# Feature-major products with high weights that walk the two halves of an activation tile in turns of two tokens

## The chip, the core and the metric

The kernel runs on one core of one Trainium2 chip, in one launch. The metric is the device time of that core in microseconds, as the median of several runs. TensorE (PE) multiplies: a matmul streams a moving operand of up to 512 columns out of SBUF through a stationary one of 128 columns, and adds the result to a bank of PSUM. VectorE (DVE), ScalarE (ACT) and GpSimd (POOL) do the elementwise work, and 16 DMA engines bring the weights from HBM.

## The reference, cut to what matters

Two blocks on one sequence of 256 tokens, 2048 features wide, in float32. The first mixes three branches (spatial gating, a state-space branch, attention to a memory), the second is a convolution block and a large feed-forward:

```python
proj = h @ w_in                                   # 2048 x 13312
a_u, a_v, a_g, b_x, b_g, x_q, x_g, gate_logits = jnp.split(proj, splits, axis=-1)
...
branch = jnp.einsum('bsnc,ncd->bsnd', ys, w_branch)
merged = jnp.sum(gates * branch, axis=2)
out = merged @ w_out
...
h = h + conformer_conv(hn, ...)                   # h @ w_pw1, taps over time, u @ w_pw2
h = h + jnp.square(jax.nn.relu(hn @ w_up)) @ w_down   # 2048 x 8192 and back
```

Nearly all of the work is products of a [256, 2048] or [256, 1024] activation with a large weight matrix, some 93 million weights in all, each used once.

## The kernel before

**Three products for one.** Each float32 operand is split into a high part, rounded to the type fp32r that TensorE takes, and a low part, the rest. A product is then high weight times high activation, high weight times low activation, and low weight times high activation. An activation is held as `HiLo` (line 275): `pair.hi` and `pair.lo`, tiles of 128 features by 256 tokens, for every 128 features k. `pair.both[:, :, k, :]` is the high and the low tile of one k together. The low tiles lie behind all the high ones, so with 16 tiles the halves of one pair are 4096 elements or 16 KiB apart in each partition; with 8 tiles (the three branch outputs and the gated branch) 8 KiB.

**Chunks.** The weights come in chunks of 128 x 1024 floats, in an order that `plan()` writes down; chunk c goes through ring `raw` (7 slots). ScalarE rounds it into ring `wh` (4 slots, line 730, semaphore `s_hi`), VectorE or GpSimd subtracts to get `wl` (lines 1132 and 661, in place of the raw chunk), and TensorE multiplies. The whole program of TensorE is written in this order, with the small matmuls of the other stages set between chunks.

**Kinds of products.** `chunk(c)` (line 2019) takes them by kind:

- "W", feature-major, the subject here: stages bx, q, k, au, ag, xg, glu, bg, out, p2 and up. The output tile is 128 features by tokens. The stationary operand is the weight tile, the moving one the activation. One `high_products` matmul (line 2005) streams the high and the low tile in one instruction of 512 columns into the two halves of a bank: columns 0 to 255 collect high times high, columns 256 to 511 high times low. One `low_products` matmul (line 2016) of 256 columns adds low weight times high activation to columns 0 to 255. A chunk has eight of each (kk 0 to 7). Every other chunk takes its low products first (`LOW_FIRST`, line 229), so eight or sixteen matmuls of one line stand in a row.
- "M", token-major (lines 2053 to 2055 and 2070 to 2072): the stationary operand is the activation, the moving one 512 adjacent weights, written to a whole bank. Stages av, v, g0, b0, g2, b2, g1, b1 and dn.
- "T" (lines 2087 to 2089): feature-major in three matmuls of 256 columns. The first chunks of bx (line 2122) and p2 (line 2154) have loops of their own, with the same 512-column form as line 2005, and "C" is a convolution with taps.

**Who takes the bank.** When a W tile is complete, ScalarE reads the second half (`half`, line 744) and VectorE adds the first (`add_half`, line 1181). Both read by column, so it matters to them which column holds what, not in which order it was written.

**A strided read elsewhere.** Two short VectorE instructions, lines 1455 and 1456, multiply 32 adjacent values of `V(7)` by 32 values of `tab[:, 1, r, :, 1]`, which are 16 elements or 64 bytes apart in each partition. Lines 1429, 1457 and 1470 are the same instruction with adjacent operands throughout, and line 1320 with 256 adjacent elements. Lines 1345 and 1347 read two elements 16 bytes apart, and line 1673 two adjacent ones.

Of the kernel before, what the change touches and what calls it, by code (L numbers as in the profile page):

```python
# [357 lines left out]
def _build(nc, a, out, ctx):  # L358
# [6 lines left out]
    def at(name, off, n, dt=F32):  # L365
        return nc.alloc_sbuf_tensor_at(name, [128, n], dt, offset=base + off)[:, :]
# [13 lines left out]
    wh = at("wh", o_wh, WN * CH, F32R).rearrange("p (s n) -> p s n", s=WN)  # L380
# [66 lines left out]
    bank = [ctx.enter_context(nc.psum_tensor(f"bank{i}", [128, 512], F32))[:, :] for i in range(8)]  # L447
# [1517 lines left out]
    def tensor(e):  # L1965
# [16 lines left out]
        def ready(per, k):  # L1982
            return k // per + 1 if per else NORMED_FOR[k]
# [13 lines left out]

        def high_products(c, j, i, s, pair, s_act, per, n0):

            dst = bank[j.banks[0]].rearrange("p (h t) -> p h t", h=2)  # L2000
            w.wait_ge(s_hi, HIGH[c])
            for kk in range(8):
                k = 8 * i + kk
                w.wait_ge(s_act, n0 + ready(per, k))
                ins = e.matmul(dst, wh[:, s, kk * 128:kk * 128 + 128], pair.both[:, :, k, :],  # L2005
                               start=i == 0 and kk == 0, stop=i == j.nch - 1 and kk == 7, skip_group_check=True)
            return ins

# [11 lines left out]
        def chunk(c):  # L2020
# [52 lines left out]
            elif j.kind == "W":  # L2073
                if c in LOW_FIRST:
                    low_products(c, j, i, r, pair, s_act, per, n0)
                    ins = high_products(c, j, i, s, pair, s_act, per, n0)
                else:
                    high_products(c, j, i, s, pair, s_act, per, n0)
                    ins = low_products(c, j, i, r, pair, s_act, per, n0)
            else:  # L2080
                dst = bank[j.banks[0]]
                for kk in range(8):
                    k = 8 * i + kk
                    w.wait_ge(s_act, n0 + ready(per, k))
                    lh = wh[:, s, kk * 128:kk * 128 + 128]
                    ll = wl[:, r, kk * 128:kk * 128 + 128]
                    e.matmul(dst[:, 0:T], lh, pair.hi[:, k, :], start=first_part and kk == 0, stop=False)  # L2087
                    e.matmul(dst[:, 0:T], lh, pair.lo[:, k, :], start=False, stop=False)  # L2088
                    ins = e.matmul(dst[:, 0:T], ll, pair.hi[:, k, :], start=False, stop=last_part and kk == 7)  # L2089
# [215 lines left out]
        for c in range(NC):  # L2305
# [4 lines left out]
            if c in (BIAS + 1, BIAS + 3):  # L2310
                h = (c - BIAS) // 2
# [5 lines left out]
            if Z <= c < Z + 4 * Z_STEP and (c - Z) % Z_STEP == 0:  # L2317
# [5 lines left out]
                for g in (2 * i, 2 * i + 1):  # L2323
                    for h in range(2):
                        o = 256 * (g % 2) + 128 * h
                        ins = e.matmul(bank[7][:, o:o + 128], vn[:, h, g * 128:g * 128 + 128], sgw[:, g, :], start=True,
                                       stop=True)
# [11 lines left out]
            if g is not None:  # L2339
                w.wait_ge(s_mg, 4 + g + 1)  # L2340
                w.wait_ge(s_m, 32)
                for n in (2 * g, 2 * g + 1):
                    if n >= 2:
                        w.wait_ge(s_mgl, n - 1)
                    for i in range(4):
                        f, h = n % 2 * 2 + i // 2, i % 2
                        ins = e.transpose(bank[4 + n % 2][:, i * 128:i * 128 + 128],
                                          gate_x[g][:, h, f * 128:f * 128 + 128], ident)
# [35 lines left out]
            if FFN + 6 <= c < FFN + 22 and (c - FFN) % 2 == 0:  # L2384
# [5 lines left out]
                for i in range(4):  # L2390
                    ins = e.transpose(bank[4 + n % 3][:, i * 128:i * 128 + 128],
                                      Xf[:, n // 2 * 4 + i, n % 2 * 128:n % 2 * 128 + 128], ident)
# [109 lines left out]
```

## Time and profile before

| | us |
|---|---|
| median of 3 runs | 1995.88 |
| lowest and highest run | 1995.85, 1995.94 |
| the profiled execution | 1996.44 |
| its span, from first to last instruction | 1994.4 |
| TensorE busy with matmuls | 1979.2 (99%), 11210 matmuls |
| VectorE busy | 1499.2 (75%) |
| ScalarE busy | 967.0 (48%) |
| GpSimd busy | 417.8 (21%) |

The time around the span is 2.0 us. A matmul's duration in the profile includes its way through the array, while the next one is already under way, so that durations of neighbours overlap. What one matmul costs in a stream is the distance from its start to the next start, and that is how the timeline is read below: so many starts between two times.

### The profile page before, as it was taken

The numbers are of one execution on the slowest core, as the hardware profiler recorded it, in microseconds if no ns is written. First come the engines' busy times: TensorE is split into PE (matmuls) and PEld (weight loads), VectorE is DVE, ScalarE is ACT, GpSimd is POOL, SyncE is SP. The second block draws the span as 40 slices with busy tenths as digits, with TensorE's granted clock in tenths as the row PEclk, the third lists the DMA queues.
The fourth block names the chain that finished last, engine by engine and source line by source line (L and its number), as shares of the span: only waits on it lengthen the run. The fifth ranks groups of instructions, "written<-read, shape, count | busy, mean of one in ns | idle before, by whom it ended". The sixth has DMA issues, their size and how long they took to land.

```text
span 1994.4 us, 28447 instructions
## 1 busy us (share of the span) xinstructions
PE 1979.2 (99%) x11210; PEld 1703.0 (85%) x11210; DVE 1499.2 (75%) x2243; ACT 967.0 (48%) x1346; POOL 417.8 (21%) x310
## 2 busy tenths in 40 slices
PE   9999999999999999999999999999999999999998
PEld 8888888888888788888899988888888888888886
DVE  7867888777799976668899996776567557656755
ACT  6555444434444345547643475554444434434443
POOL 0000234333366630000486743000000000000000
PEclk9999999999999999999999999999999999999999
DMA  9765665555665566666566656666666666666664
GB/s 327 230 181 180 186 189 172 160 159 169 181 187 182 179 190 187 192 213 190 158 175 208 191 172 183 188 198 191 191 191 189 193 195 189 192 193 190 190 192 147
DMA packets 105973, 377.45 MB, mean 189 GB/s; under 512 B 11888, under 2 KB 14448, under 8 KB 105712
## 3 DMA queue, kind: packets, MB, share of 16 engines
q1 hardware_dynamic: 105552, 375.10, 61.7%
q8 instruction: 89, 1.46, 0.3%
q10 hardware_dynamic: 288, 0.53, 0.1%
q14 instruction: 44, 0.36, 0.1%
HBM read 372.90 MB, written 2.69 MB: 188 GB/s over the span
## 4 chain that ended last, share of the span: by engine, by line
PE 82%; DVE 13%; ACT 2%; issue 2%; DMA 1%; DVEq 0%; SPq 0%; ACTq 0%
PE bank L2005 23%; PE bank L2016 12%; PE bank L2071 7%; PE bank L2072 7%; PE bank L2070 7%; DVE wl L1132 5%; PE bank L2053 4%; PE bank L2055 4%; PE bank L2054 4%; PE bank L2087 3%; PE bank L2088 3%; PE bank L2089 3%; ACT wh L730 1%; PE bank L2271 1%; DMA raw<-in_w_bxg 1%
## 5 line engine op out<-in xcount | busy, mean ns | idle before, releaser
L1132 DVE TENSOR_TENSOR wl<-raw,wh 128x1024 fp32r<-128x1024 f32 x608 | 759.5, 1254 | 375.9 <-ACT wh L730 374.3
L730 ACT ACTIVATE wh<-raw 128x1024 fp32r<-128x1024 f32 x680 | 714.1, 1057 | 627.7 <-PE bank L2072 226.3
L2005 PE MATMUL bank<-Hr,wh 128*128 128x512 f32 x1536 | 370.6, 392 | 0.2 <-DVE scrB L1181 0.2
L2005 PEld LDWEIGHTS bank<-Hr,wh 128*128 128x128 f32 x1536 | 281.5, 188 | 55.2 <-issue 0.7
L661 POOL TENSOR_TENSOR wl<-raw,wh 128x1024 fp32r<-128x1024 f32 x72 | 174.3, 2430 | 314.0 <-DVE small L1707 245.8
L2070 PE MATMUL bank<-wh,Yr 128*128 128x512 f32 x560 | 217.9, 389 | 0.0
L2071 PE MATMUL bank<-wl,Yr 128*128 128x512 f32 x560 | 217.8, 389 | 0.0
L2072 PE MATMUL bank<-wh,Yr 128*128 128x512 f32 x560 | 217.8, 389 | 0.0
L2016 PEld LDWEIGHTS bank<-Hr,wl 128*128 128x128 f32 x1536 | 197.4, 191 | 8.8 <-issue 1.1
L2005 PE MATMUL bank<-Yr,wh 128*128 128x512 f32 x832 | 201.6, 392 | 0.3 <-DVE gate_b L1202 0.3
L2016 PE MATMUL bank<-Hr,wl 128*128 128x256 f32 x1536 | 200.6, 283 | 0.0
L2005 PEld LDWEIGHTS bank<-Yr,wh 128*128 128x128 f32 x832 | 152.4, 188 | 30.4 <-DVE gate_b L1202 0.5
L2053 PE MATMUL bank<-wh,Hr 128*128 128x512 f32 x384 | 152.1, 396 | 0.1
L2055 PE MATMUL bank<-wh,Hr 128*128 128x512 f32 x384 | 149.6, 390 | 0.0
L2054 PE MATMUL bank<-wl,Hr 128*128 128x512 f32 x384 | 149.5, 389 | 0.0
L2087 PE MATMUL bank<-Hr,wh 128*128 128x256 f32 x448 | 127.5, 284 | 0.2 <-ACT scrB L839 0.2
L2088 PE MATMUL bank<-Hr,wh 128*128 128x256 f32 x448 | 126.8, 283 | 0.0
L2089 PE MATMUL bank<-Hr,wl 128*128 128x256 f32 x448 | 126.8, 283 | 0.0
L2070 PEld LDWEIGHTS bank<-wh,Yr 128*128 128x128 f32 x560 | 105.1, 188 | 21.8
L2071 PEld LDWEIGHTS bank<-wl,Yr 128*128 128x128 f32 x560 | 105.1, 188 | 21.8
L2072 PEld LDWEIGHTS bank<-wh,Yr 128*128 128x128 f32 x560 | 105.1, 188 | 21.8
L1751 DVE SCALAR_TENSOR_TENSOR bank<-upad,cst,bank 128x256 f32<-128x256 f32 x290 | 121.7, 481 | 2.3
(381 smaller groups left out, 2778.1 us busy)
## 6 DMA issues: line engine op xcount, KB each, us to landing
raw<-in_w_up SPq DMA_DIRECT2D x128, 512.0 KB, 3.6
raw<-in_w_dn SPq DMA_DIRECT2D x128, 512.0 KB, 3.5
raw<-in_w_g SPq DMA_DIRECT2D x96, 512.0 KB, 3.6
raw<-in_w_p SPq DMA_DIRECT2D x80, 512.0 KB, 3.7
raw<-in_w_b SPq DMA_DIRECT2D x48, 512.0 KB, 3.6
raw<-in_w_out SPq DMA_DIRECT2D x32, 512.0 KB, 3.6
raw<-in_w_q SPq DMA_DIRECT2D x16, 512.0 KB, 4.1
raw<-in_w_av SPq DMA_DIRECT2D x16, 512.0 KB, 3.6
```

Of the source, the lines that this page charges most:

```text
L730: e.activation(wh[:, c % WN, :], raw[:, c % RAW, :], ACT.Copy).then_inc(s_hi, 1)
L1132: e.tensor_tensor(wl[:, c % RAW, :], raw[:, c % RAW, :], wh[:, c % WN, :].bitcast(F32), ALU.subtract).then_inc(s_low_v, 1)
L2005: ins = e.matmul(dst, wh[:, s, kk * 128:kk * 128 + 128], pair.both[:, :, k, :], start=i == 0 and kk == 0, stop=i == j.nch - 1 and kk == 7, ...
L2016: ins = e.matmul(dst, wl[:, r, kk * 128:kk * 128 + 128], pair.hi[:, k, :], start=False, stop=i == j.nch - 1 and kk == 7, skip_group_check= ...
L2053: e.matmul(dst, xh, rh, start=first_part and kk == 0, stop=False)
L2054: e.matmul(dst, xh, rl, start=False, stop=False)
L2055: ins = e.matmul(dst, xl, rh, start=False, stop=last_part and kk == 1)
L2070: e.matmul(dst, xh, rh, start=first_part and kk == 0, stop=False)
L2071: e.matmul(dst, xh, rl, start=False, stop=False)
L2072: ins = e.matmul(dst, xl, rh, start=False, stop=last_part and kk == 1)
L2087: e.matmul(dst[:, 0:T], lh, pair.hi[:, k, :], start=first_part and kk == 0, stop=False)
L2088: e.matmul(dst[:, 0:T], lh, pair.lo[:, k, :], start=False, stop=False)
```

## The change

One function, `high_products`, is changed, and in it the order of one instruction's columns:

```diff
-            dst = bank[j.banks[0]].rearrange("p (h t) -> p h t", h=2)
+            dst = bank[j.banks[0]].rearrange("p (h u c) -> p u h c", h=2, c=2)
             w.wait_ge(s_hi, HIGH[c])
             for kk in range(8):
...
-                ins = e.matmul(dst, wh[:, s, kk * 128:kk * 128 + 128], pair.both[:, :, k, :],
+                ins = e.matmul(dst, wh[:, s, kk * 128:kk * 128 + 128], pair.both[:, :, k, :].rearrange("p h (u c) -> p u h c", c=2),
```

Before, the moving operand is walked as 256 tokens of the high tile and then 256 of the low one. Now it is walked as two tokens of the high tile, the same two of the low tile, the next two of the high tile and so on: 128 turns of two pairs. The output is walked in the same way, two columns in the first half of the bank, two in the second. Every product lands in the same column as before, and the number of columns, of instructions and of waits is the same.

No instruction moves on any engine. On TensorE only the form of the output differs. In the first chunks of bx, with the matmuls of line 2122 (untouched) ahead and those of lines 2005 (changed) and 2016 (untouched) in turns:

```order
 L2122 MATMUL bank<-Yr,wh 128x512 x8
 L2129 MATMUL bank<-Yr,wl 128x256 x8
-L2005 MATMUL bank<-Yr,wh 128x512 x8
+L2005 MATMUL bank<-Yr,wh 128x128x2x2 x8
 L2016 MATMUL bank<-Yr,wl 128x256 x16
```

Nothing has moved: the same eight matmuls, with their columns in 128 turns of two halves of two tokens.

## Rows read from the trace of the kernel before

**Rows 1.** Page: busy time by engine, granted clock in 40 slices, chain by engine and line.

```profile
PE 1979.2 (99%) x11210; PEld 1703.0 (85%) x11210; DVE 1499.2 (75%) x2243; ACT 967.0 (48%) x1346; POOL 417.8 (21%) x310
...
PEclk9999999999999999999999999999999999999999
...
PE 82%; DVE 13%; ACT 2%; issue 2%; DMA 1%; DVEq 0%; SPq 0%; ACTq 0%
PE bank L2005 23%; PE bank L2016 12%; PE bank L2071 7%; PE bank L2072 7%; PE bank L2070 7%; DVE wl L1132 5%; PE bank L2053 4%; PE bank L2055 4%; PE bank L2054 4%; PE bank L2087 3%; PE bank L2088 3%; PE bank L2089 3%; ACT wh L730 1%; PE bank L2271 1%; DMA raw<-in_w_bxg 1%
```

**Rows 2.** Groups of instructions: form, count, busy us, mean ns, idle before.

```profile
L2005 PE MATMUL bank<-Hr,wh 128*128 128x512 f32 x1536 | 370.6, 392 | 0.2 <-DVE scrB L1181 0.2
...
L2005 PEld LDWEIGHTS bank<-Hr,wh 128*128 128x128 f32 x1536 | 281.5, 188 | 55.2 <-issue 0.7 <-DVE scrB L1181 0.4
...
L2071 PE MATMUL bank<-wl,Yr 128*128 128x512 f32 x560 | 217.8, 389 | 0.0
...
L2005 PE MATMUL bank<-Yr,wh 128*128 128x512 f32 x832 | 201.6, 392 | 0.3 <-DVE gate_b L1202 0.3
...
L2016 PE MATMUL bank<-Hr,wl 128*128 128x256 f32 x1536 | 200.6, 283 | 0.0
...
L2016 PE MATMUL bank<-Yr,wl 128*128 128x256 f32 x832 | 110.3, 283 | 0.1
```

**Rows 3.** Timeline of TensorE, 1862 to 1870 us: start us, us, what, how many.

```profile
1862.48 2.08 PE L2016 MATMUL bank<-Hr,wl 128*128 128x256 f32 x16
1864.39 3.82 PE L2005 MATMUL bank<-Hr,wh 128*128 128x512 f32 x16
1868.05 2.08 PE L2016 MATMUL bank<-Hr,wl 128*128 128x256 f32 x16
```

**Rows 4.** Timeline of TensorE near 1600 us, token-major products.

```profile
1600.46 0.39 PE L2070 MATMUL bank<-wh,Yr 128*128 128x512 f32 x1
1600.69 0.39 PE L2071 MATMUL bank<-wl,Yr 128*128 128x512 f32 x1
...
1604.09 0.39 PE L2071 MATMUL bank<-wl,Yr 128*128 128x512 f32 x1
```

**Rows 5.** Windows: us, busy by engine (count), granted clock, DMA share, GB/s.

```profile
core 0: us, PE busy (x) PEld busy (x) DVE busy (x) ACT busy (x) POOL busy (x), PEclk, DMA share, GB/s
1862.48:1864.39 1.91, 1.91 (x17) 1.91 (x16) 1.84 (x4) 0.00 (x0) 0.00 (x0) 1.00 0.55 217
1864.39:1868.05 3.66, 3.66 (x19) 3.01 (x17) 2.22 (x4) 2.70 (x4) 0.00 (x0) 1.00 0.71 171
1600.46:1604.09 3.63, 3.63 (x18) 3.00 (x16) 2.13 (x2) 1.06 (x1) 0.00 (x0) 1.00 0.63 191
1821.50:1909.00 87.50, 87.50 (x492) 76.79 (x491) 63.24 (x92) 42.52 (x62) 0.00 (x0) 1.00 0.63 189
```

**Rows 6.** Groups of VectorE by form: busy us, mean ns, idle before.

```profile
L1320 DVE TENSOR_TENSOR scrB<-scrB,keep 128x256 f32<-128x256 f32 x64 | 27.2, 425 | 2.2
...
L1455 DVE TENSOR_TENSOR sv<-sv,tab 128x32 f32<-128x32 f32 x1 | 0.2, 211 | 0.0
L1456 DVE TENSOR_TENSOR sv<-sv,tab 128x32 f32<-128x32 f32 x1 | 0.2, 211 | 0.0
L1429 DVE TENSOR_TENSOR sv<-sv 128x32 f32<-128x32 f32 x1 | 0.2, 192 | 0.0
...
L1470 DVE TENSOR_TENSOR sv<-sv 128x32 f32<-128x32 f32 x1 | 0.2, 191 | 0.0
L1457 DVE TENSOR_TENSOR sv<-sv 128x32 f32<-128x32 f32 x1 | 0.2, 189 | 0.0
...
L1673 DVE TENSOR_TENSOR small<-small 128x2 f32<-128x2 f32 x1 | 0.2, 161 | 0.0
...
L1347 DVE TENSOR_TENSOR small<-small 128x2 f32<-128x2 f32 x1 | 0.2, 161 | 0.0
...
L1345 DVE TENSOR_TENSOR small<-small 128x2 f32<-128x2 f32 x1 | 0.2, 157 | 0.0
```

**Rows 7.** Waits: who waited for whom, total us, times, longest us.

```profile
ACT wh L730 <- PE bank L2005: 89.4, 96, 3.0
...
ACT wh L730 <- PE bank L2016: 60.2, 46, 2.7
```

## The prediction

> **What bounds the kernel now.** I read the page first: TensorE is busy for 99% of the span, VectorE for 75%, ScalarE for 48%, the clock is granted in full in every slice, and the chain that ended last goes through PE for 82%, with line 2005, the one that the change touches, at its head with 23% [rows 1]. The groups come next: line 2005 runs 1536 + 832 = 2368 times, its low partner of line 2016 as often, and the idle time before them is 0.6 us in all [rows 2]. So nothing waits for a moment at these matmuls, and each nanosecond that one of them takes more is a nanosecond more at the end. The waits say the same from the other side: ScalarE waits 89.4 and 60.2 us for lines 2005 and 2016 to give back a weight slot [rows 7].
>
> Then the timeline, for the price of one matmul in its stream. Sixteen low products start between 1862.48 and 1864.39: 1.91 us, or 119.4 ns each for 256 columns. Sixteen high products start between 1864.39 and 1868.05: 3.66 us, or 228.8 ns each for 512 columns [rows 3]. Sixteen token-major products, 512 adjacent columns each, take 1600.46 to 1604.09, 3.63 us or 226.9 ns each [rows 4]. From the two steady streams: (226.9 - 119.4) / 256 = 0.420 ns for a column, which is the upper of the two levels of TensorE's clock, 2.4 GHz, as the granted clock of 1.00 in all three windows says [rows 5], and 119.4 - 256 x 0.420 = 11.9 ns that a matmul costs whatever its length.
>
> **The change part by part.** Nothing is removed or added: as many instructions, columns and waits, and the same column gets the same sum, so no other engine's instruction changes its form, order or operands. What changes is the walk. Now the moving operand and the output each jump once in 512 columns. After, they jump at each pair, 255 times, between places 16 KiB apart in SBUF (8 KiB in the branch stages' tiles) and 1 KiB apart in the bank. The change does what it says: the output's form is 128x2x2 per partition, in one instruction.
>
> *One jump.* The high stream has one jump for each matmul and costs 228.8 ns; the token-major one has none and costs 226.9. The 1.9 ns are an upper bound of what one jump costs in the middle. It says little of 255 of them: this jump falls at the end of a tile, where the next piece of memory is a new one anyway.
>
> *A jump at every pair.* No row shows this on TensorE: all its matmuls in this kernel read and write adjacent elements, but for the jump in the middle. So I bound it. Below, it costs nothing, 0 us. A gain from it I can't exclude either, and it is a rival. Above, the nearest row is on VectorE: lines 1455 and 1456 read 32 elements of `tab` that lie 64 bytes apart and take 211 ns, while lines 1429, 1470 and 1457, the same instruction on adjacent elements, take 192, 191 and 189, on average 190.7 [rows 6]. The difference, 20.3 ns for 32 elements, is 0.63 ns each. It isn't a price of the strided form as such, since two elements 16 bytes apart take 157 and 161 ns, where two adjacent ones take 161 (lines 1345, 1347, 1673) [rows 6]. The element itself costs (425 - 190.7) / 224 = 1.05 ns by line 1320 against those of 32. So VectorE gets an element from a new place every 1.05 + 0.63 = 1.68 ns. It would not notice pairs, which it takes in 2.09 ns. TensorE would: it takes a pair in 2 x 0.420 = 0.84 ns. If its reader, too, gets to a new place only every 1.68 ns, a pair costs 1.68 in place of 0.84, and a matmul 256 x 0.84 = 215 ns more: 228.8 + 215 = 444 ns. By 2368 that is **509 us**. With 189 and 192 in place of 190.7 the step is between 1.64 and 1.73 ns, 30 us either way.
>
> I take the upper value, not 0. The ground is the match of sizes: 1.68 ns is twice 0.84, as if the memory gave a piece of 16 bytes every 1.68 ns. A stream of adjacent columns wants exactly that (four columns of 4 bytes, 4 x 0.420 = 1.68 ns), and one that uses half of each piece before it jumps wants twice that. But it is one row of another engine, and a reader that keeps the last piece of both halves would get past it.
>
> *Weighed against the notes.* The Trainium skill, Vector Engine (DVE) Microarchitecture Reference, in the part "The SBUF access granule: adjacent pairs", says that a port keeps its full rate in runs of two adjacent words and that a hop between such runs is free, while a source that hops at every element costs 1.73 ns. The second half agrees with the 1.68 worked out above; the first, carried over to TensorE, would make the term 0 in place of 509 us. What the page doesn't say is whether it holds at TensorE's rate, 2.5 times VectorE's, and no row here shows it.
>
> *Small terms.* The 1.9 ns between the two streams, 2368 x 1.9 = 4.5 us, sit in the first matmuls of a high run after a low run; in a stream twice as slow I expect them to be hidden: -4 us. The weight load of line 2005 takes 188 ns and lies beside the matmul before [rows 2]; under 444 ns it is hidden more deeply. VectorE and ScalarE work 63.24 and 42.52 us of 87.50 in the stage up [rows 5] and get more time for the same work, DMA (0.63 there) too. What is late next is still TensorE. The waits of ScalarE for a slot grow, and nobody waits for that. The token-major, three-matmul and small products don't change.
>
> Sum, on the profiled execution: 1996.4 + 509 - 4 = 2501.4; the median of the runs is 0.6 below that execution: 2501 us, of which I take **2501**.
>
> **The rivals.**
>
> *A, hops between pairs are free: 1996 us.* Each pair is one piece of memory for the reader, and one word pair for the bank, so a new place costs no more than the next one. For it: the jump in the middle costs at most 1.9 ns, and VectorE's row would be just as it is. A finer support would be two pieces held at once, since here two streams alternate, each of which moves on in order. Against it: the size of 1.68 ns. The Trainium skill, Advanced Engine Details and Errata, "Memory Cachelines", states a rule of this kind: two hits on each 16-byte line of SBUF, and every two consecutive elements adjacent in PSUM, are enough; it also says that "Any non-contiguous AP significantly slows down matmuls", which is the other side. By the one the time is 1996, by the other it is well above; no row decides between them. Range 1992 to 2000.
>
> *B, the bank pays and not the reader: 2250 us.* The output adds to what the bank holds, a read and a write for each pair. If two places that follow each other in turns get in each other's way at every second pair, a pair of 0.84 ns is paid once more for every second one: 128 x 0.84 = 107 ns, 2368 x 107 = 254 us. Nothing in the trace speaks for it or against it, since no output jumps more than once. The same slot holds anything between A and my forecast.
>
> *C, slower still: 2760 us.* The array is fed for half of the time in the high runs. If the granted clock falls to the lower level, 1.2 GHz, the high runs lose no more, but the low ones pay 256 x 0.420 = 107.5 ns more each, 2368 x 107.5 = 255 us, and 2501 + 255 = 2756. Against it: the clock stands at 1.00 throughout, and TensorE would still have a matmul under way all the time.
>
> *D, faster: 1991.4 us.* The one thing that a different walk could give back is the 4.5 us of the high runs' first matmuls. If these come from the first half of the bank, which sixteen low products in a row have just written, a high product that goes to the second half at every second pair would meet it half as hard or not at all: 1995.9 - 4.5 = 1991.4. It decides at 0.2%, or 4 us, so only if nearly all of it goes and the hops are free. Against it: it looks like a stream that catches up after short matmuls, whatever they write.
>
> **How the numbers follow.** The forecast, twice the time for the columns of line 2005, has 0.43; its own range is 2445 to 2540: 28 us down where the 11.9 ns of a matmul are hidden too (2368 x 11.9), 30 us down and up from VectorE's rows, and 4 up where the small term stays. A has 0.41, B with all between 0.08, C with all above 0.06, D 0.02. Faster by over 0.2% is D: 0.02. Within 0.2%, about what a measurement of this kernel can tell from no change, is A: 0.41. Slower is the rest: 0.57. For 8 times in 10 the range must hold both the forecast and A. It is 1992 to 2540; C and part of D stay out.
>
> **What would show it.** In the profile after, the start-to-start distance of line 2005 in a run of sixteen: about 440 ns if I am right, 227 to 229 under A, 335 under B. The low products of line 2016 at 119.4 ns say that the clock is untouched; at 227 it is C. Lines 2122 and 2154, unchanged, should keep their distance, and the token-major stages their length. The span of the stage up should grow by the share of its high products, the stage dn not at all. I am wrong if TensorE's reader or the bank holds two places at once, and nothing in this trace can tell.

## The result, and the profile after

The changed kernel takes 2240.72 us (median of 3 runs, 2240.69 to 2241.2) against 1995.88 before: a ratio of 1.1228, with a 95% interval of 1.1206 to 1.125. It is slower by 244.8 us. The direction is the forecast's, the size is not: 2501 us was forecast, and the time came out halfway, where rival B stood with 2250 us. The experiments show that B's mechanism wasn't the reason.

The page of the changed kernel, whose span is 2238.7 us (busy by engine, granted clock, chain by engine and by line):

```profile
PE 2226.2 (99%) x11210; PEld 1723.9 (77%) x11210; DVE 1502.1 (67%) x2243; ACT 973.2 (43%) x1346; POOL 405.9 (18%) x310
...
PEclk9999999999999999999999999999999999999999
...
PE 99%; DVE 0%; ACT 0%; DMA 0%; issue 0%; DVEq 0%; SPq 0%; ACTq 0%
PE bank L2005 35%; PE bank L2016 13%; PE bank L2071 6%; PE bank L2072 6%; PE bank L2070 6%; PE bank L2053 6%; PE bank L2055 6%; PE bank L2054 6%; PE bank L2087 2%; PE bank L2088 2%; PE bank L2089 2%; PE bank L2271 1%; PE bank L2122 1%; PE bank L2149 0%; PE bank L2150 0%; PE bank L2154 0%
```

Against [rows 1], the clock is granted in full throughout as before, TensorE is busy for 99% of a longer span, and the share of line 2005 in the chain goes from 23% to 35%. The chain is now PE for 99%, where it went over VectorE for 13% before: TensorE is so late that nobody else's work comes last. The other engines are busy for the same number of microseconds: VectorE 1502.1 against 1499.2, ScalarE 973.2 against 967.0. So TensorE waits for nothing new; one kind of its instructions takes longer.

The groups of instructions (busy us, mean ns, idle before):

```profile
L2005 PE MATMUL bank<-Hr,wh 128*128 128x512 f32 x1536 | 531.3, 507 | 0.0
...
L2005 PE MATMUL bank<-Yr,wh 128*128 128x512 f32 x832 | 288.2, 507 | 0.0
...
L2071 PE MATMUL bank<-wl,Yr 128*128 128x512 f32 x560 | 217.9, 389 | 0.0
...
L2016 PE MATMUL bank<-Hr,wl 128*128 128x256 f32 x1536 | 202.5, 284 | 0.0
```

Line 2005 has 531.3 + 288.2 us of busy time where [rows 2] had 370.6 + 201.6, 247.3 more. The token-major products of line 2071 have 217.9 (217.8 before) and the low products 202.5 (200.6). The timeline of TensorE in the last stage up, in the form of [rows 3]:

```profile
2110.28 2.10 PE L2016 MATMUL bank<-Hr,wl 128*128 128x256 f32 x16
2112.21 5.49 PE L2005 MATMUL bank<-Hr,wh 128*128 128x512 f32 x16
2117.53 2.10 PE L2016 MATMUL bank<-Hr,wl 128*128 128x256 f32 x16
```

Sixteen high products take 2112.21 to 2117.53, 5.32 us or 332.5 ns each, where they took 228.8. The low ones take 1.93 us, 120.6 ns each, where they took 119.4. 2368 x (332.5 - 228.8) = 245.6 us: the whole difference lies in the start-to-start distance of line 2005. The trace as a whole says the same: from each start to the next start, the 2368 high products take 789.1 us in all, where they took 545.0, which is 244.1 more. In terms of columns: 332.5 less the 11.9 ns that a matmul costs whatever its length is 320.6 ns, or 1.25 ns for each of the 256 pairs, where two columns took 0.84.

The other side of it is seen in the waits. ScalarE, which needs a weight slot back from TensorE, waits longer for line 2005 than in [rows 7]. VectorE in turn waits longer for ScalarE. None of it comes back to TensorE, which has no idle time left before these matmuls:

```profile
ACT wh L730 <- PE bank L2005: 296.7, 135, 4.3
...
ACT wh L730 <- PE bank L2016: 114.5, 59, 2.7
```

### The profile page after: what moved, and what is told of

Same layout as the page of the kernel before. It is cut to its first block, busy times and chain, and to the rows that moved or that the text cites. A ratio compares the mean times of both kernels' runs of the same rounds, so it can differ in the third digit from the quotient of the medians.

```text
span 2238.7 us, 28447 instructions
## 1 busy us (share of the span) xinstructions
PE 2226.2 (99%) x11210; PEld 1723.9 (77%) x11210; DVE 1502.1 (67%) x2243; ACT 973.2 (43%) x1346; POOL 405.9 (18%) x310
## 4 chain that ended last, share of the span: by engine, by line
PE 99%; DVE 0%; ACT 0%; DMA 0%; issue 0%; DVEq 0%; SPq 0%; ACTq 0%
PE bank L2005 35%; PE bank L2016 13%; PE bank L2071 6%; PE bank L2072 6%; PE bank L2070 6%; PE bank L2053 6%; PE bank L2055 6%; PE bank L2054 6%; PE bank L2087 2%; PE bank L2088 2%; PE bank L2089 2%; PE bank L2271 1%; PE bank L2122 1%; PE bank L2149 0%; PE bank L2150 0%; PE bank L2154 0%
## 5 line engine op out<-in xcount | busy, mean ns | idle before, releaser
L2005 PE MATMUL bank<-Hr,wh 128*128 128x512 f32 x1536 | 531.3, 507 | 0.0
L2005 PEld LDWEIGHTS bank<-Hr,wh 128*128 128x128 f32 x1536 | 292.4, 195 | 180.8 <-issue 0.9
L2005 PE MATMUL bank<-Yr,wh 128*128 128x512 f32 x832 | 288.2, 507 | 0.0
L2005 PEld LDWEIGHTS bank<-Yr,wh 128*128 128x128 f32 x832 | 158.3, 195 | 97.0 <-DVE Xf L1304 0.3
L2071 PE MATMUL bank<-wl,Yr 128*128 128x512 f32 x560 | 217.9, 389 | 0.0
L2072 PE MATMUL bank<-wh,Yr 128*128 128x512 f32 x560 | 217.9, 389 | 0.0
L2016 PE MATMUL bank<-Hr,wl 128*128 128x256 f32 x1536 | 202.5, 284 | 0.0
```

The costliest lines, as they stand in the source:

```text
L2016: ins = e.matmul(dst, wl[:, r, kk * 128:kk * 128 + 128], pair.hi[:, k, :], start=False, stop=i == j.nch - 1 and kk == 7, skip_group_check= ...
L2071: e.matmul(dst, xh, rl, start=False, stop=False)
L2072: ins = e.matmul(dst, xl, rh, start=False, stop=last_part and kk == 1)
```

## The experiments

All kernels below are the kernel before with the edit shown. Those with numbers for line 2005 (or 2016) are read like [rows 3], from the starts of sixteen matmuls in a row in the last stage up.

**Which side pays?** The change alters the walk of two operands. The first kernel walks only the moving operand in turns, with the output's columns one behind the other:

```diff
-            dst = bank[j.banks[0]].rearrange("p (h t) -> p h t", h=2)
+            dst = bank[j.banks[0]].rearrange("p (u h c) -> p u h c", h=2, c=2)
...
-                ins = e.matmul(dst, wh[:, s, kk * 128:kk * 128 + 128], pair.both[:, :, k, :],
+                ins = e.matmul(dst, wh[:, s, kk * 128:kk * 128 + 128], pair.both[:, :, k, :].rearrange("p h (u c) -> p u h c", c=2),
```

> Only the moving operand of the high products is walked in turns of two tokens; the output's 512 columns are written one behind the other. This kernel leaves out the sorting of the output: high and low sums lie mixed in the bank, so the numbers are not those of the reference. Theory R (the reader of the moving operand pays for each new place, 106.7 ns for 256 pairs): the distance in a run of line 2005 stays at 333 ns as in the changed kernel, the time near 2241 us. Theory W (the bank pays, the reader nothing): 227 to 229 ns, the time 1996 us. Theory S (the stepping through three dimensions costs on either side, or each side pays a part): between, 280 ns and 2120 us, or 333 in both this run and its counterpart.

Measured: 2240.79 us, ratio 1.1228 (1.1211 to 1.1244). Its timeline:

```profile
2112.06 5.49 PE L2005 MATMUL bank<-Hr,wh 128*128 128x512 f32 x16
2117.38 2.10 PE L2016 MATMUL bank<-Hr,wl 128*128 128x256 f32 x16
```

5.32 us for sixteen, as in the changed kernel. The counterpart leaves the reading as it was and writes in turns:

```diff
-            dst = bank[j.banks[0]].rearrange("p (h t) -> p h t", h=2)
+            dst = bank[j.banks[0]].rearrange("p (g u c) -> p u g c", g=2, c=2)
```

> The counterpart: the moving operand is streamed as before the change, high tile and then low tile, and only the output goes in pairs of columns to the two halves of the bank in turns. It leaves out the right place of the columns, so the numbers are not those of the reference. Theory R (reader): 227 to 229 ns in a run of line 2005 and 1996 us. Theory W (bank): 333 ns and 2241 us. Theory S: as in the counterpart, 280 or 333 ns in both.

Measured: 1995.64 us, ratio 1.0 (0.9991 to 1.0009).

```profile
1863.48 3.82 PE L2005 MATMUL bank<-Hr,wh 128*128 128x512 f32 x16
1867.13 2.08 PE L2016 MATMUL bank<-Hr,wl 128*128 128x256 f32 x16
```

3.65 us for sixteen, as before the change. So the reader of the moving operand pays all of it, and 255 jumps of 1 KiB in the bank cost nothing. Rival B, the bank that meets itself at every second pair, is refuted, though its time of 2250 us was right to 10 us.

**How long must a run be?** The same change with turns of 4, 8, 16 and 128 tokens on both sides; only `c=2` differs in both lines.

> The changed kernel with turns of four tokens in place of two, on both sides, so 127 jumps back and forth in place of 255 and whole pieces of 16 bytes. If each jump costs one step of the array's clock (106.7 ns / 256 = 0.42 ns), a matmul pays 53 ns: 280 ns in a run of line 2005 and 2118 us. If the price comes from pieces of 16 bytes of which only half is used, it is gone: 227 to 229 ns and 1996 us. If the bank pays once for every second pair that goes to another place, whatever lies between, 280 ns or a little less.

> Turns of eight tokens on both sides, 63 jumps. One clock step for each jump: 26.7 ns for each matmul, 253 ns in a run of line 2005, 2057 us. Pieces of 16 bytes: 227 to 229 ns, 1996 us. A threshold anywhere between two and eight tokens also shows as 1996 us here with something else at four tokens.

> The changed kernel with turns of sixteen tokens on both sides. Turns of two, four and eight tokens cost 106.7, 23 and 17 ns for each high product over 226.7. If what is left at four and eight tokens is a price for each jump that shrinks with their number, sixteen (31 jumps) give 8 ns: 235 ns in a run of line 2005 and 2010 us or so. If it is a fixed price of a walk in three dimensions, 17 ns again: 243 ns, 2027 us. If the weights' load takes part (both read the memory in the same rhythm), anything between 227 and 243.

> The changed kernel with turns of 128 tokens: four runs of columns, three jumps, but still a walk in three dimensions. Turns of 4, 8 and 16 tokens cost 23.3, 16.7 and 13.3 ns for each high product over 226.7, which is 10 ns and 0.104 ns for each of the 128, 64 and 32 runs. If the 10 ns come with the walk in three dimensions whatever its runs, 237 ns in a run of line 2005, 2368 x 10.4 = 25 us less the 4.5 of the runs' first matmuls: 2016 us. If they come from something in the short turns, 227 ns and 1996 us.

| tokens in a turn | sixteen high products, us | ns each | time, us | ratio, 95% interval |
|---|---|---|---|---|
| 2 (the change) | 5.32 | 332.5 | 2240.72 | 1.1228, 1.1206 to 1.125 |
| 4 | 4.00 | 250.0 | 2044.91 | 1.0247, 1.023 to 1.0264 |
| 8 | 3.89 | 243.1 | 2026.8 | 1.0155, 1.014 to 1.017 |
| 16 | 3.84 | 240.0 | 2019.06 | 1.0117, 1.0102 to 1.0132 |
| 128 | 3.65 | 228.1 | 1995.58 | 1.0, 0.999 to 1.0009 |
| 256 (before) | 3.66 | 228.8 | 1995.88 | |

The rows of the second and the fifth line of the table:

```profile
1916.33 4.17 PE L2005 MATMUL bank<-Hr,wh 128*128 128x512 f32 x16
1920.33 2.08 PE L2016 MATMUL bank<-Hr,wl 128*128 128x256 f32 x16
```

```profile
1863.39 3.82 PE L2005 MATMUL bank<-Hr,wh 128*128 128x512 f32 x16
1867.04 2.08 PE L2016 MATMUL bank<-Hr,wl 128*128 128x256 f32 x16
```

Nearly all of the price goes from two tokens to four, where a run fills 16 bytes, and not by half, as a price for each jump would. It doesn't vanish there: 21, 14 and 11 ns are left at 4, 8 and 16 tokens. None of the numbers expected for 4, 8 and 16 tokens came out: at 4 tokens the price lies between the 53 ns of a price for each jump and the 0 of whole pieces, and at 16 it lies between the two that were given. At 128 nothing is left, so that it isn't the form of the walk, in three dimensions, that costs.

**Does the distance matter?** The reading turns again, between the high tile of k and that of the next k, 1 KiB away, in place of the low tile 16 KiB away:

```diff
-            dst = bank[j.banks[0]].rearrange("p (h t) -> p h t", h=2)
+            dst = bank[j.banks[0]].rearrange("p (u h c) -> p u h c", h=2, c=2)
...
+            near = 8 * j.nch
...
-                w.wait_ge(s_act, n0 + ready(per, k))
-                ins = e.matmul(dst, wh[:, s, kk * 128:kk * 128 + 128], pair.both[:, :, k, :],
+                w.wait_ge(s_act, n0 + ready(per, min(k + 1, near - 1)))
+                ins = e.matmul(dst, wh[:, s, kk * 128:kk * 128 + 128], pair.hi[:, min(k, near - 2):min(k, near - 2) + 2, :].rearrange("p h (u c) -> p u h c", c=2),
```

> As the run with the reading turns alone, but the second stream is the high tile of the next k, 1 KiB further on, in place of the low tile 16 KiB further on. Left out: high weight times low activation, so the numbers are not those of the reference. If the price is one of the distance (two places 8 or 16 KiB apart that fall in the same part of the memory), it goes down or away: towards 227 ns in a run of the high products and 1996 us. If a pair from a new piece of memory costs 1.25 ns wherever it lies, it stays: 333 ns and 2241 us.

Measured: 2240.66 us, ratio 1.1228 (1.1211 to 1.1244); sixteen products take 5.32 us. The distance has no part in it:

```profile
2112.22 5.49 PE L2006 MATMUL bank<-Hr,wh 128*128 128x512 f32 x16
2117.54 2.10 PE L2017 MATMUL bank<-Hr,wl 128*128 128x256 f32 x16
```

**Turns, or half-used pieces?** The low products have one tile and 256 columns, which allows two walks that the high ones don't. First, turns of two tokens between the halves of the tile, 512 bytes apart:

```diff
-            dst = bank[j.banks[0]][:, 0:T]
+            dst = bank[j.banks[0]][:, 0:T].rearrange("p (h u c) -> p u h c", h=2, c=2)
...
-                ins = e.matmul(dst, wl[:, r, kk * 128:kk * 128 + 128], pair.hi[:, k, :],
+                ins = e.matmul(dst, wl[:, r, kk * 128:kk * 128 + 128], pair.hi[:, k, :].rearrange("p (h u c) -> p u h c", h=2, c=2),
```

> The kernel before, with turns of two tokens in the low products alone (256 columns), between the first and the second 128 tokens of the one high tile, 512 bytes apart; the output in the same turns. Each new pair at 1.25 ns in place of 0.83: 128 x 0.417 = 53 ns more, 173 ns in a run of line 2016, 2368 x 53 = 126 us, 2122 us. If 512 bytes are near enough to be free, or only 512-column instructions pay: 119.4 ns and 1996 us.

Second, always onward, every second pair and then the pairs left out:

```diff
-            dst = bank[j.banks[0]][:, 0:T]
+            dst = bank[j.banks[0]][:, 0:T].rearrange("p (u h c) -> p h u c", h=2, c=2)
...
-                ins = e.matmul(dst, wl[:, r, kk * 128:kk * 128 + 128], pair.hi[:, k, :],
+                ins = e.matmul(dst, wl[:, r, kk * 128:kk * 128 + 128], pair.hi[:, k, :].rearrange("p (u h c) -> p h u c", h=2, c=2),
```

> The kernel before, with the low products' columns taken as every second pair of tokens first (step of 16 bytes) and then the pairs left out: always onward, only one jump back, but each pair in another 16-byte piece. If the price is for a piece of which only half is used before the next, it is the same as in turns: 173 ns in a run of line 2016 and 2122 us. If it is for going back and forth between two places, it is gone: 119.4 ns and 1996 us.

Measured: 2102.56 us (1.0536, 1.052 to 1.0552) for the turns, 2251.15 us (1.128, 1.1262 to 1.1299) for the skipped pairs. The two timelines, the turns first:

```profile
1976.24 2.84 PE L2016 MATMUL bank<-Hr,wl 128*128 128x256 f32 x16
1978.91 3.81 PE L2005 MATMUL bank<-Hr,wh 128*128 128x512 f32 x16
```

```profile
2119.48 3.84 PE L2016 MATMUL bank<-Hr,wl 128*128 128x256 f32 x16
2123.15 3.82 PE L2005 MATMUL bank<-Hr,wh 128*128 128x512 f32 x16
```

Turns: 2.67 us for sixteen, 166.9 ns each, 48 more than 119.4. Skipped pairs: 3.67 us, 229.4 ns each, 110 more, though there is one jump back instead of 127 jumps to and fro. Neither expectation foresaw that the onward walk would cost over twice as much as the turns. It has the very price that the prediction took: (229.4 - 11.9) / 128 = 1.70 ns for each pair. A new theory follows. **TensorE's reader of the moving operand fetches aligned pieces of 16 bytes, one in about 1.68 ns, and keeps the last two.** Skipped pairs need a new piece each: 1.68. In turns between two streams, a pair that opens a piece pays 1.68 and its second half, two pairs later, is still there and pays 0.84: on average 1.26, and 1.25 is what the changed kernel shows. The turns of the low products come a little below it: (166.9 - 11.9) / 128 = 1.21 ns for each pair, 6 ns a matmul less than the 173 that the theory gives, and it doesn't say why.

**Tests of this theory.** Each has a number that it alone gives. Runs of four tokens, with four left out, use whole pieces; the same two tokens later breaks each run over two pieces; four streams in place of two push a piece out before its second half is asked for. The moving operand of line 2016 in the three kernels, in this order (the output is walked in the same way):

```diff
-                ins = e.matmul(dst, wl[:, r, kk * 128:kk * 128 + 128], pair.hi[:, k, :],
+                ins = e.matmul(dst, wl[:, r, kk * 128:kk * 128 + 128], pair.hi[:, k, :].rearrange("p (u e c) -> p e u c", e=2, c=4),
...
+                ins = e.matmul(dst, wl[:, r, kk * 128:kk * 128 + 128], pair.hi[:, k, 2:250].rearrange("p (u e c) -> p e u c", e=2, c=4),
...
+                ins = e.matmul(dst, wl[:, r, kk * 128:kk * 128 + 128], pair.hi[:, k, :].rearrange("p (h u c) -> p u h c", h=4, c=2),
```

> The kernel before, with the low products' columns taken in runs of four tokens with four left out between them, then the ones left out: onward in steps of 32 bytes, each run a whole aligned piece of 16 bytes. Theory P (the reader fetches aligned pieces of 16 bytes, one in 1.67 ns, which is what four columns take; every second pair skipped cost twice): each piece is used whole, so about 120 to 130 ns in a run of line 2016, the time 1996 to 2020 us. Rival J (each step to a place that isn't the next costs, 0.83 ns as with the skipped pairs): 64 steps, 53 ns more, 173 ns and 2122 us.

> As the run with runs of four tokens and four left out, but over tokens 2 to 249, so that each run of four begins in the middle of a 16-byte piece. Left out: the low weights' product for the first two and last six tokens, so the numbers are not those of the reference; 248 columns in place of 256. Theory P (aligned pieces of 16 bytes): each run touches two pieces, 124 pieces x 1.67 ns = 207 ns and what a matmul costs whatever its length, 12 to 17: about 220 ns in a run of line 2016, 2368 x 100 = 237 us more, 2230 us. Rival J (steps cost, wherever a run begins), or pieces that aren't aligned: as the aligned run.

> The kernel before, with the low products' columns taken in turns of two tokens between four streams, 64 tokens or 256 bytes apart, in place of two. Two streams cost 1.25 ns a pair, skipped pairs 1.67. Theory P2 (the reader keeps the pieces it fetched, two of them, so that with two streams every second pair is found there): with four streams each piece is gone before its second half is wanted, 128 x 1.67 = 213 ns and 12 to 17 for the matmul: 228 ns in a run of line 2016, 2250 us. Rival (a jump to another place costs 0.42 ns, however many streams): 166.7 ns and 2103 us as with two.

| walk of the low products | sixteen, us | ns each | time, us | ratio, 95% interval |
|---|---|---|---|---|
| four of eight, aligned | 1.88 | 117.5 | 1991.8 | 0.998, 0.9971 to 0.9989 |
| four of eight, from token 2, 248 columns | 3.54 | 221.3 | 2231.46 | 1.1182, 1.1163 to 1.12 |
| four streams, pairs | 3.60 | 225.0 | 2247.08 | 1.126, 1.1243 to 1.1276 |

```profile
1863.51 2.04 PE L2016 MATMUL bank<-Hr,wl 128*128 128x256 f32 x16
1865.39 3.81 PE L2005 MATMUL bank<-Hr,wh 128*128 128x512 f32 x16
```

```profile
2100.45 3.71 PE L2016 MATMUL bank<-Hr,wl 128*128 128x248 f32 x16
2103.99 3.82 PE L2005 MATMUL bank<-Hr,wh 128*128 128x512 f32 x16
```

```profile
2115.64 3.78 PE L2016 MATMUL bank<-Hr,wl 128*128 128x256 f32 x16
2119.24 3.85 PE L2005 MATMUL bank<-Hr,wh 128*128 128x512 f32 x16
```

The theory of the pieces is close in all three: 120 to 130, 220 and 228 ns were expected, 117.5, 221.3 and 225.0 measured, the first a little below its range. The rivals had 173, about 120 and 167, and are refuted. A shift of 8 bytes (with eight columns fewer) moves the same walk from 1991.8 to 2231.46 us. What the runs do not tell is whether two pieces are kept or three: four streams are too many, two are not. The four streams also lie only 256 bytes apart, a distance that no run tests with two streams. And that pieces are kept is a reading of the times: nothing in a trace shows a fetch.

**Does VectorE, from which the price was taken, behave so?** Three of its instructions in the stage up were walked in other orders, with the same results:

```diff
-                e.tensor_tensor(s, s, keep[1], ALU.mult).then_inc(s_v, w.own())
+                p2 = lambda v: v.rearrange("p (h u c) -> p u h c", h=2, c=2)
+                sk = lambda v: v.rearrange("p (u e c) -> p e u c", e=2, c=2)
+                p1 = lambda v: v.rearrange("p (h u) -> p u h", h=2)
+                e.tensor_tensor(p2(s), p2(s), p2(keep[1]), ALU.mult).then_inc(s_v, w.own())
...
-                e.scalar_tensor_tensor(s, s, 0.0, s, ALU.max, ALU.mult).then_inc(s_hm, 1)
+                e.scalar_tensor_tensor(p1(s), p1(s), 0.0, p1(s), ALU.max, ALU.mult).then_inc(s_hm, 1)
...
-                e.tensor_tensor(hid.lo[:, t % 16, :], s, hid.hi[:, t % 16, :].bitcast(F32),
+                e.tensor_tensor(sk(hid.lo[:, t % 16, :]), sk(s), sk(hid.hi[:, t % 16, :].bitcast(F32)),
```

> The kernel before, with three VectorE instructions of the stage up walked in another order on all operands, 256 columns each, the same results: line 1323 (line 1320 before, 425 ns) in pairs in turns 512 bytes apart, line 1325 (1322 before, 426 ns) in lone elements in turns 512 bytes apart, line 1328 (1325 before, 426 ns) in pairs 16 bytes apart with a pair left out between. By the 1.68 ns for a piece that the prediction took from lines 1455 and 1456: pairs in turns free, 425 ns; pairs with a step free, 426 ns, since a pair takes VectorE 2.09 ns; lone elements 0.63 ns more each if every element needs a fetch, 426 + 161 = 587 ns, and nothing more than 426 if two pieces are kept and the next three elements of each stream are found there. A rival, that VectorE keeps none, gives 587 or more for the lone elements. TensorE has slack to wait for none of them: 1996 us in all cases, up to 2010 if VectorE's longer work falls on its path.

Measured: 1995.49 us, ratio 0.9999 (0.999 to 1.0008). The groups of VectorE, with the lines moved by three:

```profile
L1325 DVE SCALAR_TENSOR_TENSOR scrB<-scrB 128x256 f32<-128x256 f32 x64 | 40.0, 625 | 2.2
...
L1328 DVE TENSOR_TENSOR Yr<-scrB,Yr 128x256 fp32r<-128x256 f32 x64 | 27.3, 427 | 31.0 <-ACT Yr L873 31.0
...
L1323 DVE TENSOR_TENSOR scrB<-scrB,keep 128x256 f32<-128x256 f32 x64 | 27.3, 426 | 2.2
```

Pairs in turns take 426 ns and skipped pairs 427, as adjacent elements do (425 and 426 before): VectorE takes a pair in 2.09 ns, which would leave time for a piece in 1.68. Lone elements in turns take 625 where 426 stood, 0.78 ns each. That is the price of a lone element again (0.63 ns by [rows 6]), or a little more, although each stream comes back to its piece. The expectation that kept pieces make lone elements free is refuted for this instruction. But it names its source twice and also writes in turns, so this run doesn't show which of its reads or writes pays, nor that VectorE keeps no piece where TensorE does.

**What is left, and a better kernel.** The aligned onward walk made the kernel 4.0 us faster than before (1991.8 against 1995.76, measured beside it), where its expectation had 1996 to 2020. More runs look at that. The first walks the moving operand of line 2016 alone; the second has the walk in the low, token-major and three-matmul products; the third and fourth in all products of 256 columns (low and three-matmul ones), in runs of four and of eight. From the second on, each product of the kind is written as here:

```diff
+        sk = lambda v: v.rearrange("p (u e c) -> p e u c", e=2, c=4)
...
-                    e.matmul(dst[:, 0:T], lh, pair.hi[:, k, :], start=first_part and kk == 0, stop=False)
+                    e.matmul(sk(dst[:, 0:T]), lh, sk(pair.hi[:, k, :]), start=first_part and kk == 0, stop=False)
```

> Runs of four tokens with four left out in the low products, on the moving operand alone; the output's columns are written one behind the other. Left out: the right place of the columns, so the numbers are not those of the reference. With both sides walked so, a low product cost 117.8 ns in place of 120.0 and the kernel 1991.8 us. If the 2.2 ns come from the reader: 117.8 ns and 1991.8 us again. If they come from the bank, where a column is then written later than the one beside it: 120.0 ns and 1996 us.

> The same walk (runs of four columns with four left out, then the ones left out), on both sides, in the low products, in all token-major products of 512 columns and in the three-matmul ones of 256 columns; the high products of line 2005 stay as before the change. If a matmul gains 2.2 ns wherever its columns are taken so: 3600 + 1344 more of them, 4944 x 2.2 = 11 us less, 1981 us. If a walk in three dimensions costs 512-column matmuls 10 ns as it does the high products: 3600 x 10 = 36 us more for these and 3 less for the others, 2025 us.

> The version that the experiments point to: the kernel before, with runs of four columns and four left out in all 256-column products of fp32r (low products and three-matmul products, lines 2018 and 2089 to 2091), on both sides. The 512-column products stay as before. The low products gain 2.2 ns each (1991.8 us); with the same walk the three-matmul ones took 53.4, 52.7 and 52.6 us from start to start in place of 54.4, 53.7 and 53.2, which is 2.6 us less: 1989 us. If the gain of the three-matmul ones was only the other stages' shift, 1991.8 us.

> As the run before with runs of eight columns, two whole 16-byte pieces, and eight left out. If what the walk gains comes from taking a piece from another place each time, eight gain half as much or nothing: 117.8 ns becomes 119 to 120 in a run of the low products and the time 1992 to 1996 us. If any onward walk in three dimensions gains it, as with four: 1989 us.

| kernel | time, us | ratio, 95% interval |
|---|---|---|
| reading only, low products | 1991.73 | 0.998, 0.9972 to 0.9989 |
| low, token-major and three-matmul products | 2004.57 | 1.0044, 1.0032 to 1.0057 |
| all 256-column products, runs of four | 1988.88 | 0.9966, 0.9952 to 0.9979 |
| all 256-column products, runs of eight | 1988.57 | 0.9964, 0.9952 to 0.9977 |

The gain lies with the reader (1991.73 us without touching the output's order). It adds up over the 256-column products, and runs of eight give as much as runs of four. For 512 columns the sign turns: the token-major products with this walk, lines 2072 to 2074 there, take 3.70 us for sixteen, 231.3 ns from start to start, where [rows 4] had 226.9. That is 4 ns each, neither the gain of 2 nor the loss of 10 of the expectation, whose 1981 and 2025 us were both missed:

```profile
1609.70 0.40 PE L2072 MATMUL bank<-wh,Yr 128*128 128x512 f32 x1
...
1613.40 0.39 PE L2073 MATMUL bank<-wl,Yr 128*128 128x512 f32 x1
```

Why a walk of whole pieces gains 2 ns at 256 columns and costs 4 at 512, and why turns of 4 to 16 tokens keep a price of 11 to 21 ns, stays open. The best kernel of the study is the last, 7.1 us or 0.36% below the kernel before.

## Why the prediction was right or wrong

*What bounds the kernel: right.* Each nanosecond of line 2005 came out at the end: 103.7 ns for each of 2368 matmuls are 245.6 us, and the time went up by 244.8. Nothing else took part to speak of: the low products changed by about 1 ns each, the clock and VectorE's busy time stayed as they were, and behind the last high product the token-major stage dn takes 95.1 us, where it took 95.0, as the prediction said.

*A jump at every pair: the right side pays, but not at every pair.* This is the step that failed, 509 us of which 245 came. The prediction took from VectorE's lines 1455 and 1456 that a new place costs 1.68 ns, and charged it for every pair: 444 ns for a high product, where 332.5 were measured, or 1.25 ns a pair. Where every pair needs a piece of its own, the price is right: skipped pairs take 1.70 ns. But by the theory of the pieces, in turns between two streams only every second pair does. The text named the very way past it, "a reader that keeps the last piece of both halves", and treated it as all or nothing: under it, rival A would have been right with 1996 us. Keeping the pieces, by the theory, saves the second fetch of each and not the wait for the first, which a pair of 0.84 ns can't cover. (1.68 + 0.84) / 2 = 1.26 ns in place of 0.84, by 256 pairs, is 108 ns, 2368 of them 255 us: with this the forecast would have been 2247, against 2240.72. There was some luck in the price, too. It came from single elements on VectorE, and when VectorE took single elements in turns, they cost 0.78 ns more each, 1.83 and not 1.68 ns. That the two engines share one cause is not shown.

*The row of one jump was rightly set aside:* at a tile's end a jump is free, and three jumps of 128 tokens are, too.

*Weighed against the Trainium skill.* The Trainium skill's rule for VectorE ("The SBUF access granule: adjacent pairs" in Vector Engine (DVE) Microarchitecture Reference), that hops between runs of pairs are free, holds for VectorE here, with 426 and 427 ns. Carried over to TensorE, as rival A did, it is wrong, by 1.25 ns a pair in turns and 1.70 in steps against 0.84. Of the Trainium skill's two rules in "Memory Cachelines" (Advanced Engine Details and Errata), the one on 16-byte lines agrees with the size of the piece, but two hits on a line are not enough for TensorE with fp32r (1.70 ns for a skipped pair): only all four of a line in a row bring the price down, from 104 to 21 ns in turns and to nothing in the onward walk. The one on PSUM, that "Any non-contiguous AP significantly slows down matmuls", no run here bears out: pairs in turns in the bank cost nothing (1995.64 us); single columns were not tried.

*Small terms.* The 4.5 us at the head of the high runs were expected to be hidden, and they were. Before, the matmuls of line 2005 start 226.7 ns apart from the tenth of a run of sixteen on, but about 228 to 236 ns apart for the second to the fifth. After, both are at 333.3 to 333.6. So the steady price of the turns is 106.7 ns and not 103.7, and the hidden heads give the difference back. The low products paid 1.8 us in all (285.2 us before, 287.0 after, from start to start), which the prediction didn't have. One token-major line, 2055, took 1.9 us less; the two cancel.

*The rivals.* A is refuted by the time and by the run with the reading turns. B had the number, 2250 us, by luck, and a mechanism that the run with the writing turns refutes: a right time is no proof of a reason. C didn't come: the clock stayed at 1.00. D didn't come in this form, though a walk of the moving operand does give back some microseconds.

## What to carry to other kernels

By the theory of the pieces, an fp32r matmul that streams a column each 0.42 ns uses all that its reader can fetch, one aligned 16-byte piece in 1.68 ns. So let the moving operand run through whole, aligned pieces, and, where it turns between places, through runs of 128 tokens and not of 16; the output may go in pairs to the two halves of its bank in turns for nothing. When a price is carried from one engine to another, ask how many fetches the access really needs, with what was fetched before still at hand, and charge for each of them, before choosing between all and nothing.

## What the runs showed that was not expected

The two sides of a matmul are unlike: the same 255 jumps cost 104 ns on the reading side and 0 on the writing side. In a walk of four tokens with four left out, eight bytes of misalignment cost the low products 104 ns each (117.5 to 221.3). The distance of the jumps, 512 bytes, 1 KiB or 16 KiB, made little or no difference: 0.37 ns for each of 128 pairs at 512 bytes, 0.41 for each of 256 at the others. And adjacent columns are not the fastest walk of a 256-column matmul: runs of four with as many left out take 117.5 ns against 119.4, and with runs of eight in all products of 256 columns the kernel was 0.36% faster.
